# More block-product tiles in the feed-forward stages, and ScalarE's copies of a pair moved ahead of the late tile's high part

## The reference

```
u, g = split(h2 @ w_up)
u = causal_dwconv(u, w_conv, b_conv)      # three taps along the positions
x = x + gate2 * ((silu(u) * g) @ w_down)
```

```
x = x + (silu(h @ w_gate) * (h @ w_up)) @ w_down
```

## Time and profile before

| what | value |
|---|---|
| runs | 2884.59, 2885.97, 2886.22 us; median 2885.97 |
| the profiled execution's own time | 2884.7 us |
| its span, first to last instruction | 2882.9 us |
| instructions | 36572, of which 15275 matmuls |
| mean granted clock of TensorE | 0.998 of full |
| TensorE busy | 2845.5 us |
| VectorE busy | 1533.2 us |
| ScalarE, GpSimd busy | 1157.6, 1139.4 us |

### The profile page before, as it was taken

How to read it: one execution, slowest core, us unless ns; L and a number is a source line. 1 busy time by engine, 2 the same in 40 slices (tenths; PEclk the granted TensorE clock), 3 DMA queues, 4 the chain that set the end, 5 groups by cost and what they waited for, 6 DMA issues and landing times.

```text
span 2882.9 us, 36572 instructions
## 1 busy us (share of the span) xinstructions
PE 2845.5 (99%) x15275; PEld 2389.0 (83%) x15275; DVE 1533.2 (53%) x2156; ACT 1157.6 (40%) x1761; POOL 1139.4 (40%) x470
## 2 busy tenths in 40 slices
PE   8999999999999999999999999999999999999999
PEld 5777888888888887788898888888889877788888
DVE  6444572466665524422266755648556456575563
ACT  4335333342333424532243434344334466443333
POOL 2332345334444332344435343544343433334332
PEclk9999999999999999999999999999999999999999
DMA  8331363346564421233233333333333322233332
GB/s 258 104 104 50 106 194 110 95 150 201 191 197 123 126 74 52 76 97 98 81 105 97 102 99 97 94 99 94 107 97 96 110 59 74 74 93 106 95 103 73
DMA packets 507289, 314.20 MB, mean 109 GB/s; under 512 B 14291, under 2 KB 478837, under 8 KB 506869
## 3 DMA queue, kind: packets, MB, share of 16 engines
q1 hardware_dynamic: 507124, 311.87, 36.6%
HBM read 309.73 MB, written 2.10 MB: 108 GB/s over the span
## 4 chain that ended last, share of the span: by engine, by line
PE 94%; DVE 3%; ACT 1%; SPq 1%; DMA 1%; issue 0%; POOL 0%; DVEq 0%; ACTq 0%
PE b L494 17%; PE b L496 16%; PE b L495 16%; PE o L494 4%; PE o L496 4%; PE o L495 4%; PE s L495 3%; PE s L496 3%; PE s L494 3%; PE b L1225 2%; PE b L1224 2%; PE b L1223 2%; PE b L1162 1%; PE b L1164 1%; PE b L1163 1%; PE s L1225 1%
## 5 line engine op out<-in xcount | busy, mean ns | idle before, releaser
L3363 POOL TENSOR_TENSOR lo<-raw,hi 128x1024 fp32r<-128x1024 f32 (+2 forms) x460 | 1137.1, 2481 | 1713.8 <-ACT hi L1500 1428.8
L1500 ACT ACTIVATE hi<-raw 128x1024 fp32r<-128x1024 f32 (+2 forms) x463 | 474.9, 1035 | 307.8 <-DMA raw<-in_w_up_dram 91.5
L494 PE MATMUL b<-HH,hi 128*128 128x512 f32 x1400 | 558.2, 399 | 0.0
L496 PE MATMUL b<-HH,lo 128*128 128x512 f32 x1400 | 545.7, 390 | 0.0
L495 PE MATMUL b<-HL,hi 128*128 128x512 f32 x1400 | 545.7, 390 | 0.0
L494 PEld LDWEIGHTS b<-HH,hi 128*128 128x128 f32 x1400 | 262.9, 188 | 61.7 <-issue 7.1
L496 PEld LDWEIGHTS b<-HH,lo 128*128 128x128 f32 x1400 | 262.8, 188 | 56.1
L495 PEld LDWEIGHTS b<-HL,hi 128*128 128x128 f32 x1400 | 263.1, 188 | 53.9 <-issue 1.4
L2899 DVE TENSOR_TENSOR FL<-CB,FH 128x512 fp32r<-128x512 f32 x88 | 115.8, 1316 | 61.6 <-ACT FH L1994 61.6
L2513 DVE SCALAR_TENSOR_TENSOR AA<-raw,CA,AA 128x512 f32<-128x512 f32 x140 | 139.7, 998 | 3.3
L494 PE MATMUL b<-FH,hi 128*128 128x512 f32 (+1 forms) x362 | 132.7, 366 | 0.0
(11 more groups left out here) (641 smaller groups left out, 6375.1 us busy)
## 6 DMA issues: line engine op xcount, KB each, us to landing
raw<-in_w_up_dram SPq DMA_DIRECT2D x88, 512.0 KB, 4.0
raw<-in_w_ada_dram SPq DMA_DIRECT2D x80, 512.0 KB, 4.8
raw<-in_w_in_dram SPq DMA_DIRECT2D x76, 512.0 KB, 3.9
raw<-in_w_mg_dram SPq DMA_DIRECT2D x48, 512.0 KB, 3.7
raw<-in_ffn_w_gate_dram SPq DMA_DIRECT2D x44, 512.0 KB, 3.9
raw<-in_ffn_w_up_dram SPq DMA_DIRECT2D x44, 512.0 KB, 3.8
raw<-in_w_down_dram SPq DMA_DIRECT2D x32, 448.0 KB, 3.5
raw<-in_ffn_w_down_dram SPq DMA_DIRECT2D x32, 448.0 KB, 3.5
```

Source lines behind the costliest of these rows:

```text
L494: e.matmul(out, wh, xh, start=start and k == 0, stop=False)
L496: mm = e.matmul(out, wl, xh, start=False, stop=stop and k == last)
L1500: e.activation(t["hi"][:, c % NSLOT, 0:w], K.raw[:, c % NSLOT, 0:w], ACT.Copy).then_inc(*m.hi.up(c))
L3363: e.tensor_tensor(t["lo"][:, s, 0:w], K.raw[:, s, 0:w], t["hi"][:, s, 0:w].bitcast(F32), ALU.subtract).then_inc(*m.lo.up(n))
```

## The change

Three things. FFN 1 gets 13 pairs, FFN 2 and 3 get 14 each, 41 in all for 29. They stand in runs: (5,) 6, 7 | 8, 9, 10 | 12, 13, 14 | 15, 16, 17 | 19, 20, where | is a down projection or a direct tile; 21 is direct now, and in FFN 1 the first pair is 6 in place of 7. On ScalarE `ffn_high` leaves `late_tile`: behind a pair it comes after the `pair_copies` of the next pair, before a direct tile and a down projection it stays where it was. The last call of ScalarE's `late_tile`, with nothing to do now, is removed. VectorE, TensorE, GpSimd and SyncE follow the tables.

```diff
--- before.py
+++ after.py
@@ -41,8 +41,9 @@
 
 
 
-PAIRS_OF = ((), (7, 8, 10, 12, 14, 15, 17, 19, 21), (5, 7, 8, 10, 12, 14, 15, 17, 19, 21),
-            (5, 7, 8, 10, 12, 14, 15, 17, 19, 21))
+PAIRS_OF = ((), (6, 7, 8, 9, 10, 12, 13, 14, 15, 16, 17, 19, 20),
+            (5, 6, 7, 8, 9, 10, 12, 13, 14, 15, 16, 17, 19, 20),
+            (5, 6, 7, 8, 9, 10, 12, 13, 14, 15, 16, 17, 19, 20))
 HEAD = 4
 ROOM = 8
 DOWN = {7: (0, 7), 14: (7, 7)}
@@ -2045,7 +2046,6 @@
                 self.pair_high(i, g, part)
         if f is not None:
             self.ffn_silu(i, f)
-            self.ffn_high(i, f)
 
     def ffn(self, i):
 
@@ -2058,8 +2058,10 @@
         late = None
         for f in range(HEAD, KF):
             self.late_tile(i, late, ffn_next(i, f) if f not in DOWN else None)
-            late = None
             if f not in PAIRS_OF[i]:
+                if late is not None:
+                    self.ffn_high(i, late)
+                    late = None
                 for j in (2 * f, 2 * f + 1):
                     yield from self.tile()
                     self.ffn_jobs(i, j)
@@ -2069,20 +2071,23 @@
                 yield BUSY
                 yield BUSY
                 self.pair_copies(i, f)
+                if late is not None:
+                    self.ffn_high(i, late)
                 yield BUSY
                 self.split(n + AHEAD)
                 yield BUSY
                 late = f
             if f in DOWN:
                 self.late_tile(i, late, None)
-                late = None
+                if late is not None:
+                    self.ffn_high(i, late)
+                    late = None
                 g = ffn_next(i, f)
                 for d in range(KD):
                     if g is not None and d >= KD - 2:
                         for part in ((0, 1) if d == KD - 2 else (2,)):
                             self.pair_high(i, g, part)
                     yield from self.tile()
-        self.late_tile(i, late, None)
```

## The result

The changed kernel takes 2890.9 us (median of 20 runs, 2888.0 to 2892.8) against 2884.6 us of the kernel before in the same session (20 runs, 2883.0 to 2886.5): ratio 1.0019, 95% interval 1.0013 to 1.0026. Its profiled execution took 2891.15 us with a span of 2889.4 us, 6.5 more than the 2882.9 of before. So twelve more tiles are made with fewer products, and the kernel is a little slower.

The account below looks back on a forecast made before the run. TensorE, 99% busy, was taken as the bound. Saved 9.7 + 3.0 = 12.7, paid 10.8 + 6.8 = 17.6: net +4.9 on 2884.7 = 2889.6, plus 1.3 to the runs' median: 2890.9 us, range 2885 to 2896.

Parts of the forecast that it names:

- What an extra pair saves: TensorE, FFN 1 to 3: a pair takes 10.07 us, a direct tile 10.88; twelve more pairs save 9.7 us.
- What moving the last pair saves: Down projections behind FFN 2 and 3: with tile 21 direct, waits of 0.8 and 2.2 us go, 3.0 saved.
- FFN 1, start of pair 6: TensorE idles 3.7 us at pair 6's first product, waiting for GpSimd's split, with VectorE 0.04 us ahead at the port.
- Its sixth product: FFN 1, pair 6: sixth product waits 3.0 us for ScalarE's copy; pair 7's is late by 0.6.
- Pairs 12, 13, 19, 20: FFN 1: sixth products late by 0.9, 0.8, 0.9 and 0.9 us, together 3.5.
- FFN 2 and 3: Sixth products at pairs 5, 12 and 19 late by 1.2, 1.1 and 1.1 us in each FFN, 6.8 together.
- The new order: ScalarE's copies before the late high part: costs nothing itself; the old order would add 44 us over three FFNs.
- Bounds: Port order of VectorE and GpSimd unknown: net -7.7 us if they never block, +13.4 if GpSimd always comes first.
- The clock: Rival: TensorE's granted clock drops after the 3.7 us idle, costing 1.7 to 3.4 us: 2892.6 to 2894.3; chance 0.15.
- GpSimd first: Rival: GpSimd first at the port at pairs 6, 7, 13, 20: always 2899.4 us, chance 0.10; half 2895.1, 0.05.
- Little blocking: Rival: VectorE and GpSimd hardly block and VectorE keeps up, savings earned nearly whole: 2878.3 us; chance 0.10.
- cheaper pairs: Rival: on TensorE a 256-column product costs 0.1135 us, a pair 9.53, 6.5 more saved: 2884.4 us; chance 0.05.

Follow-up runs that it names:

- spread_set: Changed kernel with other pair sets: 35 pairs, tile 21 direct, ScalarE's new order kept; 2879.72 us, ratio to the kernel before 0.998.
- tile21_only: Kernel before with tile 21 direct in FFN 1 to 3, all else as it was; 2883.41 us beside 2886.05 of before.
- copies_first: Changed kernel, with ScalarE making the pair's own copies before the next pair's high parts at pairs 5 and 12; 2892.05 us beside 2886.09 of before.
- order_only: Kernel before's pair sets with the changed kernel's ScalarE order alone; 2885.22 us beside 2886.05 of before.
- old_order: Changed kernel with ScalarE's old order, the late tile's high part ahead of the next pair's copies; 2950.77 us beside 2886.09 of before.
- port_order: Changed kernel, with VectorE's first low part of pair 6 in FFN 1 waiting for GpSimd's split; 2891.14 us beside 2886.09 of before.
- both repeats: Two intended set edits that by a slip ran the changed kernel unaltered; 2891.18 us, ratio 1.0017, and 2890.66 us, ratio 1.0018, to before.
- from_7: Changed kernel with tile 6 of FFN 1 direct, so its first pair is 7; 2887.33 us, ratio 1.0003 to before.
- spread_old_order: Changed kernel with the 35-pair sets of spread_set and ScalarE's old order together; 2912.17 us.

## Why the prediction was right

The forecast was 2890.9 us and the median is 2890.9. That it meets to the tenth is luck: the change was put at +4.9 us, and the medians differ by 6.3 (the spans by 6.5, of which 1.2 lie before anything that the change touches), while the three runs of before that it started from had a median 1.3 us above that of all twenty. The two errors cancel. The stretches of the table that the change touches, each within 0.5 us, are not luck. By its own steps:

- *What an extra pair saves*: held. The page's 432 more instructions and 7.5 us less busy TensorE go with it (the busy figure, whose ends are modelled, is no exact check on 9.7); `spread_set`'s FFN 1, two pairs more and no wait, gives 0.77 each for 0.81. A pair in the new trace takes 10.08 us (1605.05 to 1615.13) as before.
- *What moving the last pair saves*: held. Forecast 3.0; the two stretches behind FFN 2 and FFN 3 are 1.1 + 2.5 = 3.6 us shorter, and `tile21_only` shows the two waits gone by that edit alone.
- *FFN 1, start of pair 6*: 3.7 forecast; 3.54 listed, and VectorE ahead by 0.04 us as assumed. (A listed wait is 0.16 us less than the product's lateness: due at 1528.76 + 10.88 = 1539.64, it started at 1543.34, 3.70 late. The forecasts are latenesses.)
- *Its sixth product*: 3.0 forecast; 2.71 listed. Pair 7's was to be late by 0.6 and is by 0.3.
- *Pairs 12, 13, 19, 20*: 0.9, 0.8, 0.9, 0.9 forecast; 0.80, 0.45, 0.79, 0.42 listed, 0.95, 0.61, 0.95 and 0.58 late. The first of each couple is right, the second was put too high by 0.2 and 0.3; which of its steps was too long isn't shown. Its order of events held: ScalarE's Silu of tile 12 waits for VectorE until 1663.95, and the copy of pair 13 stands behind it at 1664.49. Each restart costs 0.1 more (the first product of 256 columns takes 0.39 instead of 0.28), so FFN 1 as a whole paid 7.4 + 4 x 0.81 = 10.6 for 10.8.
- *FFN 2 and 3*: 1.2, 1.1, 1.1 forecast; 1.03, 1.00, 0.99 listed, 3.7 with lateness and restarts for 3.4 in each. `copies_first` shows that ScalarE's own order isn't behind it, and ScalarE's row at pair 5 that VectorE's sum is.
- *The new order*: costs nothing that shows (`order_only`), and without it these sets lose 60 us (`old_order`), where 44 were forecast: the waits are 39.4, the clock wasn't counted. That was the one term that was short by much; it wasn't in the sum.
- *Bounds*: the lower one supposed that VectorE and GpSimd never block each other. The held rows of 3.37 and 3.39 against 1.22 and 2.35 in `port_order` exclude it.

**The rivals.** *The clock* (2): the fall came in both repeats and not in the profiled run, right behind the 3.5 us, and hid in the next wait, the case that the text had priced at nothing; in `port_order` it came elsewhere and cost about 1.7. The argument against it, that 2.2 us in FFN 3 had left the clock at 1.00, holds for that one execution only: in `order_only` the same wait had 0.50 behind it. So part of the case may be in the median, by the estimate above 2.6 us at most, and which part isn't shown. *GpSimd first* (3): it was VectorE by 0.03 to 0.05 us at each of the places that the case named in FFN 1, pairs 6, 7, 13 and 20, and at 6, 13 and 20 of FFN 2 and 3. `port_order` shows that forcing the other order there moves the stall from the first product to the sixth. GpSimd first at every place, the rival's far end, was not tried. *Little blocking* (4) and *cheaper pairs* (5) fell: the waits are there, and a pair takes seven times 1.44 us as before. The rule of the Trainium skill, "TensorE: Matmul & The Clock Gate", section "Back-to-back issue gap", gives N/2.4 + 2.5 ns as the gap of isolated matmuls. In this kernel's stream it isn't borne out: a pair takes 10.08 us and not the 9.17 of the rule, and where the sum would have ended at +0.3 us by it, the measured 0.13% to 0.26% is 3.7 to 7.5 us.

What stays open: FFN 0 and the attention parts differ by a microsecond or two between executions of one program, and `from_7`'s median is 2 us above what its stretch in FFN 1 gives (2886.05 x 1.0019 - 6.4 = 2885.1). That goes with the clock: its four runs at 0.998 have a mean of 2884.4 us, its six at 0.996 or 0.997 one of 2888.0. Where the clock fell in those six no trace shows.

## What to carry to other kernels

An engine that is 99% busy makes each microsecond of its work worth a microsecond only while its feeders keep up place by place. Here six more pairs brought their gain and twelve gave back more than they brought, though VectorE is idle for 44% of the span. Ask of each new place when its producers finished the last job, not how busy they are on the whole. A choice of the places (35 pairs, with tile 21 direct) beat both fewer (29) and more (41). An order of work on a feeder that is neutral today can be what the next step stands on: test it with the old sets and with the new, as both answers are needed.

## What the runs showed that was not expected

- The granted clock is no property of a program: behind one and the same idle of 3.5 us it halved in two executions of the changed kernel and stayed full in one, behind one and the same wait of 2.2 us it stayed full in the kernel before and halved in `order_only`, and in `old_order` and `spread_old_order` it took up to 24 and 15 us of losses of 60 and 34. Idle time of TensorE among its products can cost more than its length.
- It can also cost nothing: with the next wait 7 us away, the execution at half the clock and the one that waited 2.7 us at full clock came out alike to 0.02 us (110.98 and 111.00).
- A forced order at a shared port moved a stall and removed none, though each single operation came out shorter: 2.35 + 1.22 instead of 3.39 + 3.37.
